# Feed-forward and embedding gate read the residual without its norm, and a row of norm factors is multiplied in at the tile's exit

## What is computed

```python
def rms_norm(x, g):
    y = x * rsqrt(mean(x * x, axis=-1) + EPS)
    return y * g
...
h = h + token_mixers(rms_norm(h, g_mix_norm[i]), ...)
h = h + conv_ffn(rms_norm(h, g_ffn_norm[i]), w_up[i], conv_w[i], conv_b[i], w_down[i])
ple_gate = sigmoid(rms_norm(h, g_ple_norm[i]) @ w_ple_gate[i])
h = h + ple_gate * (p[i] @ w_ple_proj[i])
...
def conv_ffn(u, w_up, conv_w, conv_b, w_down):
    up = u @ w_up                       # 1024 -> 5632
    conv = conv_b + sum(pad(up)[:, j:j + length] * conv_w[j] for j in range(3))
    gate, val = split(conv, 2)
    return (gelu(gate) * val) @ w_down  # 2816 -> 1024
```

## Time and profile before

| | us |
|---|---|
| median of 3 runs | 2754.01 |
| lowest, highest | 2746.56, 2760.47 |
| span of the profiled execution | 2756.3 |
| time of the profiled execution around its span | not shown |
| TensorE busy with products | 2588.3 |
| VectorE busy | 1462.2 |
| ScalarE busy | 1085.0 |

### The profile page before, as it was taken

The page is one execution under the profiler, slowest core; times in us unless marked ns, Lnnn a source line. Parts: engine busy times, 40 slices in busy tenths (PEclk is TensorE's granted clock), DMA queues, the critical chain, the costliest instruction groups (busy, mean ns, idle before and its releaser), DMA issues.

```text
span 2756.3 us, 35741 instructions
## 1 busy us (share of the span) xinstructions
PE 2588.3 (94%) x14616; PEld 1908.2 (69%) x14616; DVE 1462.2 (53%) x2520; ACT 1085.0 (39%) x1725; POOL 155.8 (6%) x133
## 2 busy tenths in 40 slices
PE   5999999999999989999999999999999989999777
PEld 4777677888877777777888877666766658733226
DVE  4787556545546698555646455445434525422227
ACT  3436544333334435654424233344322324233235
POOL 1410000000000320000000000000000000022210
PEclk9999999999999999999999999999999989899998
DMA  4322232223221332232232222312111124699991
GB/s 152 115 81 85 88 123 99 92 93 106 88 96 56 124 100 90 86 118 97 94 105 92 92 92 91 118 46 88 49 50 43 36 96 145 243 371 394 400 366 75
DMA packets 70283, 342.97 MB, mean 124 GB/s; under 512 B 11618, under 2 KB 12514, under 8 KB 37220
## 3 DMA queue, kind: packets, MB, share of 16 engines
q1 hardware_dynamic: 64996, 332.22, 33.8%
q0 software_dynamic: 5120, 8.40, 0.9%
HBM read 312.26 MB, written 28.31 MB: 124 GB/s over the span
## 4 chain that ended last, share of the span: by engine, by line
PE 79%; DVE 9%; SPq 4%; ACT 4%; DMA 3%; issue 2%; POOLq 0%; DVEq 0%; ACTq 0%
PE bank L900 15%; PE bank L902 15%; PE bank L901 15%; SPq L3356 4%; PE bank L1090 4%; PE bank L1091 3%; PE bank L1092 3%; PE bank L2326 2%; PE bank L3223 2%; PE bank L1134 2%; DVE wl L1345 1%; PE bank L1164 1%; PE bank L1154 1%; DMA raw<-in_WE 1%; PE bank L2313 1%
## 5 line engine op out<-in xcount | busy, mean ns | idle before, releaser
L900 PE MATMUL bank<-XH,wh 128*128 128x512 f32 x1328 | 526.9, 397 | 14.1 <-DVE XL L1386 9.9
L901 PE MATMUL bank<-XL,wh 128*128 128x512 f32 x1328 | 519.3, 391 | 0.0
L902 PE MATMUL bank<-XH,wl 128*128 128x512 f32 x1328 | 519.2, 391 | 0.0
L1345 DVE TENSOR_TENSOR wl<-raw,wh 128x2048 fp32r<-128x2048 f32 (+1 forms) x165 | 367.2, 2227 | 156.8 <-ACT wh L1867 156.7
L1867 ACT ACTIVATE wh<-raw 128x2048 fp32r<-128x2048 f32 (+1 forms) x165 | 303.5, 1841 | 176.9 <-DMA raw<-in_W 176.8
L900 PEld LDWEIGHTS bank<-XH,wh 128*128 128x128 f32 x1328 | 249.7, 188 | 89.7 <-DVE XL L1386 19.5
L902 PEld LDWEIGHTS bank<-XH,wl 128*128 128x128 f32 x1328 | 249.8, 188 | 53.9
L901 PEld LDWEIGHTS bank<-XL,wh 128*128 128x128 f32 x1328 | 250.2, 188 | 50.9 <-issue 0.2
L900 PE MATMUL bank<-arena_rounded,wh 128*128 128x512 f32 x576 | 229.4, 398 | 5.3 <-DVE arena_rounded L1581 3.2
L902 PE MATMUL bank<-arena_rounded,wl 128*128 128x512 f32 x576 | 228.4, 396 | 0.0
L901 PE MATMUL bank<-arena_rounded,wh 128*128 128x512 f32 x576 | 228.3, 396 | 0.0
(11 more groups left out here) (529 smaller groups left out, 3989.2 us busy)
## 6 DMA issues: line engine op xcount, KB each, us to landing
raw<-in_W SPq DMA_DIRECT2D x153, 1024.0 KB, 4.9
arena<-in_WE SPq DMA_DIRECT2D x31, 1024.0 KB
wh_full<-in_WE SPq DMA_DIRECT2D x15, 1024.0 KB
raw<-in_WE SPq DMA_DIRECT2D x15, 1024.0 KB
gsave<-scr SPq DMA_DIRECT2D x48, 256.0 KB
scr<-gsave SPq DMA_DIRECT2D x48, 256.0 KB, 3.9
XH_full<-in_WE SPq DMA_DIRECT2D x10, 1024.0 KB
XL_full<-in_WE SPq DMA_DIRECT2D x10, 1024.0 KB
```

The costliest lines, as they stand in the source:

```text
L900: pe.matmul(ps[0:c.stop - c.start, :], h[:, k, c], hi, start=i == 0, stop=False)
L901: pe.matmul(ps[0:c.stop - c.start, :], h[:, k, c], lo, start=False, stop=False)
L902: mm = pe.matmul(ps[0:c.stop - c.start, :], l[:, k, c], hi, start=False, stop=i == len(xs) - 1)
L1345: w_lo.inc(dve.tensor_tensor(wl[:, i % 3, 0:k], raw[:, i % 3, 0:k], wh[:, i % 3, 0:k].bitcast(F32), ALU.subtract), i)
```

## The change

The operand of up and gate products is no longer the normed residual but the residual times the gain, split into QH and QL, which lie in the arena where uh and ul were. Both halves are made while the tiles of hT come in. The row of norm factors is copied from its bank to RROW once per norm, and every up tile and every gate tile is multiplied by it when VectorE takes it out of its bank, into one of three places in SBUF (UP, or PS for the gate). ScalarE's and VectorE's convolution terms read that place and not the bank; the convolution of a tile, by `convolve`, follows one tile later than before, and the low half of the hidden tile (`hidden_low`) with it. Hidden halves are now in XH and XL. On TensorE `two_tiles` is gone: the sums stand after the first up tile, the spread after the second; in the gate stage embed tiles 0 to 3, sums, embed 4 and 5, spread, embed 6 and 7. `keep_warm` is left out in r = 1, 2, 4, 5. The norms r = 0, 3 and 6 are as before.

```diff
-        uh, ul = R3(0, 8), R3(4096, 8)
+        QH, QL = R3(0, 8), R3(4096, 8)
+        RROW, UP = S_(5), [S_(3), S_(4), S_(6)]
...
-                keep_warm(ps, 0 if r == 0 else 1 if r % 3 else 3)
+                keep_warm(ps, 3 if r and r % 3 == 0 else 0)
...
-                            if q == 0 and which == 0:
-                                two_tiles([("up", li, 0, 0, i) for i in range(2)], weights(n, 256), lambda k: x((3 * li + 1, k)))
-                            else:
-                                for i in range(2):
-                                    tile(("up", li, q, which, i), weights(n, 256), slice(128 * i, 128 * i + 128), xs)
+                            for i in range(2):
+                                first = q == 0 and which == 0
+                                tile(("up", li, q, which, i), weights(n, 256), slice(128 * i, 128 * i + 128), xq,
+                                     (lambda k: x((3 * li + 1, k))) if first and i == 0 else None)
+                                if first:
+                                    (norm_row if i else norm_sums)(3 * li + 1)
...
-                    ks = [(k, uh[:, k, :], ul[:, k, :]) for k in range(cn)]
+                    ks = [(k, XH[:, k, :], XL[:, k, :]) for k in range(cn)]
...
-                rms(3 * li + 2, embed(li, n0 + 61))
+                embedded = embed(li, n0 + 61)
+                embedded(0, 4)
+                norm_sums(3 * li + 2)
+                embedded(4, 6)
+                norm_row(3 * li + 2)
+                embedded(6, 8)
```

VectorE:

```diff
+            def low_of(r, gain, k):
+
+                dve.wait_ge(*xh((r, k)))
+                x.inc(dve.scalar_tensor_tensor(out=QL[:, k, :], in0=hT[:, k, :], scalar=K(gain, k),
+                                               in1=QH[:, k, :].bitcast(F32), op0=ALU.mult, op1=ALU.subtract), (r, k))
+
+            def norm_row(r):
+
+                root(("sum", r), 4, 1.0 / D, EPS, normcols(r), nroot, r, nrec)
+                key = ("spread", r)
+                dve.wait_ge(*bank.full(key))
+                bank.emptied(dve.tensor_copy(RROW, bank.ap(key)), key)
+                dve.wait_ge(*bank.empty(key))
...
                     bank.emptied(ins, key)
+                    if k:
+                        low_of(r, f"gffn{r // 3}", k - 1)
                     if k >= 2:
                         add_to_norm(r, k - 1)
+                low_of(r, f"gffn{r // 3}", 7)
...
+                def convolve(ci, j, q, which, i):
+
+                    f = FIRST[ci] + j + i + 22 * which
+                    u = up_place(q, which, i)
+                    s = (FV if which else FG)[q % 2][i]
+                    dve.wait_ge(*aff((li, q, which, i)))
+                    v.inc(dve.scalar_tensor_tensor(out=s[:, 1:T], in0=u[:, 0:T - 1], scalar=K(f"cw1{li}", f), in1=s[:, 1:T],
+                                                   op0=ALU.mult, op1=ALU.add))
+                    dve.wait_ge(*v())
+                    ins = dve.scalar_tensor_tensor(out=s[:, 2:T], in0=u[:, 0:T - 2], scalar=K(f"cw0{li}", f), in1=s[:, 2:T],
+                                                   op0=ALU.mult, op1=ALU.add)
+                    if which == 0:
+                        conv.inc(ins, (li, q, i))
+                        return
+                    v.inc(ins)
+                    dve.wait_ge(*v())
+                    dve.wait_ge(*gelu((li, q, i)))
+                    fmul.inc(dve.tensor_tensor(s, s, FG[q % 2][i], ALU.mult), (li, q, i))
...
                             for i in range(2):
+                                key = ("up", li, q, which, i)
+                                u = up_place(q, which, i)
+                                dve.wait_ge(*bank.full(key))
+                                bank.emptied(dve.tensor_tensor(u, bank.ap(key), RROW, ALU.mult), key)
+                                dve.wait_ge(*bank.empty(key))
                                 if i:
                                     cuts_to(n + 1)
...
+                                if which or i:
+                                    convolve(ci, j, q, *divmod(2 * which + i - 1, 2))
+                                elif j:
+                                    convolve(ci, j - 2, q - 1, 1, 1)
+                                    hidden_low(j - 2, q - 1, 0)
+                                if j and not which and i:
+                                    hidden_low(j - 2, q - 1, 1)
                         q += 1
+                    convolve(ci, cn - 2, q - 1, 1, 1)
+                    for i in range(2):
+                        hidden_low(cn - 2, q - 1, i)
...
+                def gated(k):
+                    s = PS[k % 3]
+                    dve.wait_ge(*ple_on((m, k)))
...
+                    pmul.inc(dve.tensor_tensor(s, s, pp[:, k, :], ALU.mult), (m, k))
+                    dve.wait_ge(*pmul((m, k)))
+                    ple_h.inc(dve.tensor_tensor(hT[:, k, :], hT[:, k, :], s, ALU.add), (m, k))
+                    if k >= 2:
+                        add_to_norm(r, k - 1)
...
+                    key = ("ple", m, k)
+                    dve.wait_ge(*bank.full(key))
+                    bank.emptied(dve.tensor_tensor(PS[k % 3], bank.ap(key), RROW, ALU.mult), key)
+                    if k:
+                        gated(k - 1)
+                gated(7)
```

More of the change, by code:

```diff
@@ L564, in program @@
         nrec = Signal(sem("nrec"), ALLN)
-        u_done = Signal(sem("u_done"), [(r, k) for r in ALLN for k in range(8) if r >= 6 or k < 7])
+        u_done = Signal(sem("u_done"), [(r, k) for r in (0, 3, 6) for k in range(8) if r >= 6 or k < 7])
         xkeys = []
@@ L606, in program @@
         fmul = Signal(sem("fmul"), gelu.order)
+        conv = Signal(sem("conv"), gelu.order)
         u_hi = Signal(sem("u_hi"), gelu.order)
@@ L935, in tensor_engine @@
             xs = [(k, XH[:, k, :], XL[:, k, :]) for k in range(KT)]
+            xq = [(k, QH[:, k, :], QL[:, k, :]) for k in range(KT)]
             def column_sums(key, src, cols, ready):
@@ L1673, in ffn @@
-                                key = ("up", li, q, which, i)
-                                s = (FV if which else FG)[q % 2][i]
-                                dve.wait_ge(*bank.full(key))
-                                dve.wait_ge(*aff((li, q, which, i)))
-                                v.inc(dve.scalar_tensor_tensor(out=s[:, 1:T], in0=bank.ap(key)[:, 0:T - 1],
-                                                               scalar=K(f"cw1{li}", f), in1=s[:, 1:T], op0=ALU.mult, op1=ALU.add))
@@ L1698, in ffn @@
                         bank.emptied(dve.tensor_tensor(hT[:, k, :], bank.ap(key), hT[:, k, :], ALU.add), key)
+                        if ci == 2 and k:
+                            low_of(3 * li + 2, f"gple{li}", k - 1)
                         if ci == 2 and k >= 2:
@@ L1898, in rms @@
                     high((r, k), k, U[k % 3], u_ready(r, k))
-                    if between is not None and k == 0:
-                        between()
             def layer_norm(r, bname, j, split=True):
@@ L2039, in out_linear @@
                         cuts_to(n0 + k // 2 + 2)
+                    high_of(r, f"gffn{r // 3}", k)
                     square_of(r, k)
+                root(("sum", r), normcols(r), nroot, r)
             def p_split(m):
@@ L2050, in ffn, with hidden_high, gelu_of @@
                 p_split(li)
+                def hidden_high(ci, j, q, i):
+                    act.wait_ge(*fmul((li, q, i)))
+                    if ci and j == 0:
+                        act.wait_ge(*bank.full(("down", li, ci - 1, 7)))
+                    u_hi.inc(act.activation(XH[:, j + i, :], FV[q % 2][i], ACT.Copy), (li, q, i))
+                def gelu_of(q, i):
+                    act.wait_ge(*conv((li, q, i)))
+                    gelu.inc(act.activation(FG[q % 2][i], FG[q % 2][i], ACT.Gelu_apprx_tanh), (li, q, i))
                 for ci, cn in enumerate(FCH):
@@ L2081, in ffn @@
                         if ci == 2:
+                            high_of(3 * li + 2, f"gple{li}", k)
                             square_of(3 * li + 2, k)
+                embedded(li, 0, 4)
+                root(("sum", 3 * li + 2), normcols(3 * li + 2), nroot, 3 * li + 2)
+                embedded(li, 4, 8)
             def ple(m, n0, r):
```

108 lines of the change are left out of this document (36 added, 72 removed).

## The result

The changed kernel takes 2785.33 us in the median of four runs (2783.61 to 2789.47), beside 2753.7 for the kernel before: 1.0114 times, 95% interval 1.0093 to 1.0134. It is slower, as forecast, but by 31.6 us and not by 19.4, and its time lies 1.3 us above the stated range.

The account below looks back on a forecast made before the run. TensorE, busy 94% of the span, was taken as the bound. Terms -25.2 + 23.8 + 8.4 + 7.6 + 3.8 + 1.0 = +19.4 us gave a median of 2773.4 us, range 2757 to 2784.

Parts of the forecast that it names:

- Part 1: At r = 1, 2, 4 and 5, the norm leaves TensorE's path and warm-ups go: -25.2 us.
- the rival of a norm still on the path: TensorE waits at k = 7 for a late low(7), half the norm gain lost: +12, 2786 us, chance 0.04.
- Part 2: In the up stage, each tile's added VectorE row product is hidden in mid-chunk, VectorE at 74%: cost 0.
- Part 3: At six chunk ends, TensorE waits for late hidden low halves behind VectorE's split and convolutions: +23.8 us.
- Part 4: Behind the six chunk-end holes TensorE's clock falls, 1.4 us each: +8.4 us, bounds 0 and 10.2.
- Part 5: Up and gate operands move to the slower arena, hidden operands to faster XH, XL: +7.6 us, bounds 0 and 13.7.
- The rival by which the place doesn't matter: Operand location leaves product spacing unchanged, as the skill page says: 11.8 in all, 2766 us, chance 0.13.
- Part 6: At the gate's end, r = 3 and 6, delayed gating makes sums wait: +3.8 us, +1.0 for a clock fall.
- both slow rivals: VectorE becomes the up stage's bound, 2795 us, chance 0.07; the norm stays on the path, 2786 us, chance 0.04.
- The rival on the faster side (2741 us): At chunk ends the hidden layer comes in time, so holes and their clock falls vanish: -12.8, chance 0.12.
- the one with VectorE as the bound in the up stage: VectorE and ScalarE waits add up, splits come late at 44 block borders: +22, 2795 us, chance 0.07.

Follow-up runs that it names:

- experiment 6: Changed kernel with four warm-up products on TensorE in each of the six chunk-end holes, which fit into them: 2775.02 us, 1.0078.
- experiment 12: Changed kernel with split last and convolution in turn at chunk ends, first two down tiles together, early embedding gating, arena 128 bytes further: 2725.77 us, 0.9905.
- experiment 1: Changed kernel with VectorE's next weight split moved behind the two hidden low halves in each chunk's last pair: 2771.43 us, 1.0048.
- experiment 2: Changed kernel with value tile 0's convolution done before VectorE waits for value tile 1's bank in each chunk's last pair: 2769.97 us, 1.0055.
- experiment 7: Changed kernel with 128 bytes per partition left free ahead of the arena, so it starts at a multiple of 2048 bytes: 2766.66 us, 1.0043.
- experiment 10: Changed kernel with tile 6's gating done before VectorE waits for tile 7's bank, in the embedding gate's last tile only: 2788.99 us, 1.0126.
- experiment 11: Changed kernel with each embedding-gate tile gated before the wait for the next bank, and the stage's last split behind the last gating: 2782.77 us, 1.0124.
- experiment 8: Kernel before the change with 128 bytes per partition left free ahead of the arena: 2747.68 us, 0.9974.
- experiment 9: Kernel before the change with XH and XL moved to start 384 bytes past a multiple of 2048, all else in place: 2778.51 us, 1.0091.
- experiment 3: Changed kernel with both the weight split moved behind the low halves and value tile 0's convolution done earlier at chunk ends: 2757.04 us, 0.9994.
- experiment 4: Changed kernel with TensorE doing each chunk's first two down tiles together, the last hidden pair last, VectorE and ScalarE untouched: 2751.75 us, 0.9975.
- experiment 5: Changed kernel with nine warm-up products on TensorE in each of the six chunk-end holes, which overfilled them: 2793.79 us, 1.0161.

## Why the prediction was right and wrong

By its own steps, in us, from the two profiled executions. Of the rows that one trace can't separate, the clock's is from experiment 6, the restarts are what its down stages keep beyond those of experiment 12, and the place is the remainder of the +22.2 of both layers; the last row is all that differs behind the gates.

| step | forecast | measured |
|---|---|---|
| 1, norm off the path | -25.2 | -24.4 |
| 2, row product in mid-chunk | 0 | 0 |
| 3, holes at chunk ends | +23.8 | +23.3 |
| 3, restarts behind the holes | not in the sum | +1.6 |
| 4, clock behind the holes | +8.4 | +12.2 |
| 5, place of the operands | +7.6 | +9.5 |
| 6, gate's end, and all behind it | +4.8 | +5.8 |
| sum | +19.4 | +28.0 |

**Part 1 was right.** r = 1 and 4: 13.31 us each, of which 0.28 belongs to the place, so 6.0 and 5.1 saved. r = 2 and 5, from the last down product to the end of the gate, take 58.35 us where they took 870.47 - 807.39 = 63.08 and 64.70; with 1.1 for the place that is 5.8 and 7.5. No wait for low(7) appeared; the rival of a norm still on the path falls.

**Part 2 was right.** VectorE is busy for 39.40 of the 55 us from 460 to 515, 72%, and TensorE for all 55:

```profile
460.00:515.00 55.00, 55.00 (x238) 44.58 (x237) 39.40 (x46) 24.96 (x26) 0.00 (x0) 1.00 0.28 96
```

**Part 3 was right**, chain and size: 3.93 and 3.97 in chunks of eight, 4.8 in those of six, less the 2.1 of before. Experiments 1 and 2 took out its two halves one by one. Missing from it was that a down stage loses some 0.3 us more per hole: in experiment 6, at full clock, the six take 267.3 us, of which 239.4 are products at the pace of experiment 12 and 26.3 warm-ups and rest. Where the 1.6 us that are left go wasn't looked into.

**Part 4 is the term that was mis-sized**, 8.4 us where experiment 6 measured 12.2. The mechanism was as told: six holes, six falls. But the price was taken from falls of 3.4 us behind shorter holes, and the upper bound of 10.2 assumed that none lasts longer. Five of the six lasted 6.8 us. They began within the hole, and with the first one, which began behind it, 27.3 us of half clock lay outside the holes. In the window from 673.20 to 678.10 twelve products took 4.90 us, where 12 x 0.2267 = 2.7 would do; at that rate 27.3 us cost 12.1, an estimate that agrees with the experiment. The rows of before held no hole of 4 us in this part, and a bound taken from shorter ones was no bound. Nor does the hole fix the fall: in experiment 7 four of the six lasted 3.4 us, in 10 and 11 all six 6.8, so this term has a spread of its own that the range left out.

The Trainium skill says in the section that the prediction names ("TensorE: Matmul & The Clock Gate", "Part 1: The HAM clock gate") that the low level is the default and activity releases it. The traces agree: at the six holes the clock fell when TensorE stood idle and stayed at 1.00 when warm-ups filled them.

**Part 5 was right** with its choice against the page, and 1.9 us too low: the slow spacing in "up" is 0.2326 to 0.2333 us, and 0.2321 was taken. Up tiles went to 5.58 us and down tiles to 5.44, as VectorE reads them:

```profile
553.73 0.69 DVE L1730 TENSOR_TENSOR hT<-bank,hT 128x512 f32<-128x512 f32 x1 [1.79 <-PE bank L905]
559.17 0.69 DVE L1730 TENSOR_TENSOR hT<-bank,hT 128x512 f32<-128x512 f32 x1 [4.75 <-PE bank L905]
```

And experiments 7, 8 and 9 moved the spacing by the address alone, in both directions. The rival by which the place doesn't matter is refuted here. So is, for these products, the rule of the Trainium skill ("TensorE: Matmul & The Clock Gate", section "Back-to-back issue gap") that the gap goes by the column count: at 512 columns and full clock the runs show 0.2267 and 0.2325 to 0.2333.

**Part 6** had its place right and its path incomplete: at r = 6 the sums begin at 1745.31, 4.6 us after the last gate tile is in its bank, as forecast; at r = 3 at 886.34, 5.7 us after it, by the split that nobody had moved but that ScalarE's late square held up. A queue one engine further on was not followed. Against 2.7 before, the waits are 3.0 and 1.9 us longer. The +5.8 of the table is not a measurement of them: it is 2.3 us in the stretch from r = 3 to the end of "out" and 3.5 behind r = 6, and in the traces of seven kernels that are alike in these stretches (the changed one and experiments 1 to 6) the first takes from 412.8 to 420.4 us, the second from 1038.3 to 1057.4. Experiment 11 removed the waits without a gain that can be seen. So what part 6 costs is not shown, and that 5.8 stands so near to 4.8 is luck.

**The rest of the miss** lies between executions. The profiled execution of the changed kernel took 2784.43 us, 0.9 less than the median; its span was 26.8 us longer than that of before, and the medians differ by 31.6. The span of before, from which the sum started, was 2756.3, and the median of its runs 2753.7, while what lies around a span was 1.3 us in the changed kernel. So that execution was probably some 4 us slow. The sum's +19.4 on the median therefore missed 28.0 by 8.6, and the difference of the medians by 12.2; 3.6 of that is the spread of the runs, and the interval of the ratio (25.6 to 36.9 us) holds both. The range was too narrow above: it left out both slow rivals and added only 4 us for the latencies of part 3 and the spread of the runs. The 8.6 us are 3.8 for the clock, 1.9 for the place, 1.6 for the restarts, 0.8 for a norm that gave less, 1.0 from the stretches behind the gates, less 0.5 for the holes.

The rival on the faster side (2741 us) falls with the holes, the one with VectorE as the bound in the up stage with the windows.

## What to carry over

A row that is added to an engine with slack is free only where nobody waits for that engine's last result: list, for each end of a stage, what stands in its queue between the last input and the value that the next stage starts with, and put long work that isn't due (here a 2.3 us weight split) behind it. An idle hole of TensorE is to be priced with the half-clock time behind it, here half as much again, and the cheapest mend can be on the waiting side, with work that needs no late value. When an operand moves to another tensor, look at the spacing of the products that read it, not only at their count.

## What the runs showed of the hardware

- The spacing of 128x128 by 128x512 products of rounded float32 depends on the start of the moving operand: 0.2267 us at a multiple of 2048 bytes (up and down products in experiments 7 and 12), 0.2325 to 0.2333 at 1920 and at 384 past one. 128 bytes of padding gained 19 us in one kernel and 7 in the other, and XH and XL moved to a slow start cost 25. Which starts are bad, and why, wasn't tried further.
- A product of plain float32 operands of the same shape shows as two passes of 0.407 us at full clock (experiment 5: 18 in 7.32 us).
- At holes of 3.9 to 4.8 us the granted clock was 0.50 for 3.4 or 6.8 us, parts of it inside the hole: for 6.8 in five of six cases in the changed kernel, in two of six in experiment 7, in all six in 10 and 11. At holes of 2.6 and 3.1 us in experiments 1 and 2 it was either, at those of 1.7 to 1.9 us in experiments 1 to 3 it fell for 3.4 us or not at all. In these stages it cost about 0.45 us for each us of half clock outside a hole, an estimate from the changed kernel's window with 12 products in 4.90 us.
